# A chunk's k-blocks in twos: four high products in a row, then four low products

## The reference

```
x = x + 0.5 * SwiGLU_1(RMSNorm(x))
u = RMSNorm(x) @ w_in            # 2048 x 6144
   group A: differential attention, 4 heads; group B: stick-breaking attention, 8 heads
x = x + concat(A_out, B_out) @ w_out
x = x + 0.5 * SwiGLU_2(RMSNorm(x))
x = RMSNorm(x)
_swiglu(x) = (silu(x @ w_gate) * (x @ w_up)) @ w_down
```

## Time and profile before

| | us |
|---|---|
| median of 3 runs | 1893.87 |
| lowest run | 1893.20 |
| the profiled execution | 1893.42 |
| span of that execution, first to last instruction | 1891.6 |
| PE busy / its weight loads | 1875.1 / 1638.4 |
| DVE busy | 1133.5 |
| ACT busy | 902.9 |
| POOL busy | 16.7 |

### The profile page before, as it was taken

How to read it: one execution, slowest core, us unless ns; L and a number is a source line. 1 busy time by engine, 2 the same in 40 slices (tenths; PEclk the granted TensorE clock), 3 DMA queues, 4 the chain that set the end, 5 groups by cost and what they waited for, 6 DMA issues and landing times.

```text
span 1891.6 us, 28251 instructions
## 1 busy us (share of the span) xinstructions
PE 1875.1 (99%) x10792; PEld 1638.4 (87%) x10792; DVE 1133.5 (60%) x1303; ACT 902.9 (48%) x1213; POOL 16.7 (1%) x18
## 2 busy tenths in 40 slices
PE   8999999999999999999999999999999999999998
PEld 7888888888888888888888888888888888888887
DVE  7665556555555667565655566655555565556565
ACT  7444434444344446554656455444344444344454
POOL 0000000000000000100000000000000000000000
PEclk9999999999999999999999999999999999999999
DMA  9555655555555556554445555556555556655553
GB/s 306 180 197 181 197 178 195 184 197 180 181 196 186 186 167 216 179 173 162 157 161 172 172 185 180 197 182 196 178 195 183 197 179 187 191 192 185 176 172 119
DMA packets 344098, 349.91 MB, mean 185 GB/s; under 512 B 5984, under 2 KB 342112, under 8 KB 344032
## 3 DMA queue, kind: packets, MB, share of 16 engines
q1 hardware_dynamic: 343456, 348.02, 56.6%
q10 hardware_dynamic: 576, 0.96, 0.1%
HBM read 346.85 MB, written 2.10 MB: 184 GB/s over the span
## 4 chain that ended last, share of the span: by engine, by line
PE 61%; issue 38%; DVE 0%; DMA 0%; ACT 0%; POOLq 0%; POOL 0%; DVEq 0%
PE psum L1164 38%; PE psum L1169 19%; PE psum L1250 1%; PE psum L1253 0%; PE psum L1402 0%; DVE x_res L1118 0%; DMA param_sb<-in_params 0%; PE psum L1336 0%; PE psum L1347 0%; PE psum L1362 0%; PE psum L1393 0%; PE psum L1201 0%; PE psum L1394 0%; PE psum L1363 0%; PE psum L1346 0%
## 5 line engine op out<-in xcount | busy, mean ns | idle before, releaser
L1164 PE MATMUL psum<-x_split,w_split 128*128 128x512 f32 x3008 | 931.7, 395 | 0.0
L726 DVE TENSOR_TENSOR w_split<-w_raw,w_split 128x1024 fp32r<-128x1024 f32 (+1 forms) x664 | 766.5, 1196 | 252.3 <-ACT w_split L442 246.6
L442 ACT ACTIVATE w_split<-w_raw 128x1024 fp32r<-128x1024 f32 (+1 forms) x664 | 651.3, 1030 | 320.2 <-PE psum L1169 318.8
L1169 PEld LDWEIGHTS psum<-x_split,w_split 128*128 128x128 f32 x3008 | 551.8, 188 | 124.8
L1169 PE MATMUL psum<-x_split,w_split 128*128 128x256 f32 x3008 | 578.0, 279 | 0.0
L1164 PE MATMUL psum<-h_split,w_split 128*128 128x512 f32 x1640 | 507.1, 395 | 0.0
L1164 PEld LDWEIGHTS psum<-x_split,w_split 128*128 128x128 f32 x3008 | 465.4, 189 | 8.1
L1169 PEld LDWEIGHTS psum<-h_split,w_split 128*128 128x128 f32 x1640 | 300.4, 188 | 67.7
L450 ACT ACTIVATE lo_sum<-psum 128x512 f32<-128x512 f32 x159 | 95.0, 597 | 507.1 <-PE psum L1164 507.1
L1169 PE MATMUL psum<-h_split,w_split 128*128 128x256 f32 x1640 | 314.6, 279 | 0.0
L1164 PEld LDWEIGHTS psum<-h_split,w_split 128*128 128x128 f32 x1640 | 254.0, 189 | 4.8
(11 more groups left out here) (140 smaller groups left out, 530.9 us busy)
## 6 DMA issues: line engine op xcount, KB each, us to landing
w_raw<-in_ffn_gate SPq DMA_DIRECT2D x86, 1024.0 KB, 5.0
w_raw<-in_ffn_up SPq DMA_DIRECT2D x86, 1024.0 KB, 5.0
w_raw<-in_ffn_down SPq DMA_DIRECT2D x64, 1024.0 KB, 5.5
w_raw<-in_w_in SPq DMA_DIRECT2D x48, 1024.0 KB, 5.2
w_raw<-in_ffn_down SPq DMA_DIRECT2D x32, 768.0 KB, 4.8
w_raw<-in_w_out SPq DMA_DIRECT2D x16, 1024.0 KB, 5.5
x_res<-in_x_t SPq DMA_DIRECT2D x8, 256.0 KB, 6.9
w_raw<-in_ffn_gate SPq DMA_DIRECT2D x8, 256.0 KB, 7.0
```

Source lines behind the costliest of these rows:

```text
L442: nc.scalar.activation(w_split[:, slot % 2, 0, h * half:(h + 1) * half], w_raw[:, slot, h * half:(h + 1) * half], ACT.Copy).then_inc(hi_ma ...
L726: nc.vector.tensor_tensor(w_split[:, slot % 2, 1, part], w_raw[:, slot, part], w_split[:, slot % 2, 0, part].bitcast(F32), ALU.subtract).t ...
L1164: return mm(psum[:, 2 * j + b, :], one, other, start=first, stop=last)
L1169: return mm(psum[:, 2 * j + b, 256:512], one, other, start=False, stop=False)
```

## The change

`chunk` takes its k-blocks two at a time. For the k-blocks k0 and k0 + 1 it issues the four highs (k0 with b = 0 and 1, then k0 + 1 with b = 0 and 1), then the four lows in the same order. In the last pair of a strip's second chunk the four lows come first and the four highs last. `high` and `low` now take the k-block as an argument. The waits on `lo_made` by half and on `block_ready` are made at the even k-blocks; they stood there before as well, since `block_ready` names even k-blocks only and the halves start at even ones. `first_body` and `merged_chunk` are not touched.

```diff
--- before.py
+++ after.py
@@ -1149,34 +1149,34 @@
                 if not by_half:
                     pe.wait_ge(lo_made, lo_value(c))
                 w = w_split[:, slot % 2, :, 0:kn * STRIP].rearrange("p l (k n) -> p l k n", n=STRIP)
-                for k in range(kn):
-                    if by_half and k % (kn // 2) == 0:
-                        pe.wait_ge(lo_made, lo_value(c) - (k == 0))
-                    if block_ready is not None and block_ready(k) is not None:
-                        pe.wait_ge(*block_ready(k))
+
+                def high(k, b):
+                    cols = slice(b * P, (b + 1) * P)
                     a = left(k)
-                    first = not second and k == 0
-                    last = second and k == kn - 1
-
-                    def high(b):
-                        cols = slice(b * P, (b + 1) * P)
-                        one, other = (a[:, 0, cols], w[:, :, k, :]) if still else (w[:, 0, k, cols], a)
-                        return mm(psum[:, 2 * j + b, :], one, other, start=first, stop=last)
-
-                    def low(b):
-                        cols = slice(b * P, (b + 1) * P)
-                        one, other = (a[:, 1, cols], w[:, 0, k, :]) if still else (w[:, 1, k, cols], a[:, 0, :])
-                        return mm(psum[:, 2 * j + b, 256:512], one, other, start=False, stop=False)
-                    if last:
-                        low(0)
-                        low(1)
-                        high(0)
-                        ins = high(1)
+                    one, other = (a[:, 0, cols], w[:, :, k, :]) if still else (w[:, 0, k, cols], a)
+                    return mm(psum[:, 2 * j + b, :], one, other, start=not second and k == 0, stop=second and k == kn - 1)
+
+                def low(k, b):
+                    cols = slice(b * P, (b + 1) * P)
+                    a = left(k)
+                    one, other = (a[:, 1, cols], w[:, 0, k, :]) if still else (w[:, 1, k, cols], a[:, 0, :])
+                    return mm(psum[:, 2 * j + b, 256:512], one, other, start=False, stop=False)
+                for k0 in range(0, kn, 2):
+                    if by_half and k0 % (kn // 2) == 0:
+                        pe.wait_ge(lo_made, lo_value(c) - (k0 == 0))
+                    if block_ready is not None and block_ready(k0) is not None:
+                        pe.wait_ge(*block_ready(k0))
+                    four = [(k, b) for k in (k0, k0 + 1) for b in range(2)]
+                    if second and k0 == kn - 2:
+                        for k, b in four:
+                            low(k, b)
+                        for k, b in four:
+                            ins = high(k, b)
                     else:
-                        high(0)
-                        high(1)
-                        low(0)
-                        ins = low(1)
+                        for k, b in four:
+                            high(k, b)
+                        for k, b in four:
+                            ins = low(k, b)
                 ins.then_inc(chunk_used, 1)
 
             def x_block(second):
```

## The result

The changed kernel took 1900.84 us (median of 6 runs, 1900.40 to 1901.61) against 1893.71 for the kernel before (median of 6). The ratio is 1.0036, with a 95% interval of 1.0027 to 1.0046: slower, by 7.1 us between the medians, clear of the scatter and far inside the 2% that was named. One of the six runs of the kernel before took 10671.68 us and is left out of the ratio; without it that kernel's median is 1893.55. The forecast was 1903.7 with 1895 to 1915, a loss of 9.8 us.

A forecast was written before the change was run, and what follows sets the result against it. PE was taken as bound by distances between matmul starts. Span 1891.6 plus 9.8 us for lows and 0 for highs gave 1901.4, with 1.8 around it 1903.2; on the median of 1893.87, 1903.7 us, range 1895 to 1915.

The forecast's parts named there:

- PE's spacing is the bound, and nothing else moves.: On PE, distances between matmul starts set the time; the two old waits and the work of other engines stay.
- Count of long lows, 2580, at 0.1200 against 0.1162.: In chunks, 2580 more lows stand third or later in their row, at 0.1200 instead of 0.1162 us: 9.8 us.
- Highs: 0 ... I take 0, the value of the rows of four.: In chunks, highs in longer rows cost 0.2325 us each as in pairs: 0, with rows of eight -3 to +3 us.
- behind a high, a low or two start a little sooner: In rows of lows, the first two cost 0.1162 us each, and from the third on a low costs 0.1200.
- Rival 1: In rows of four lows, each low costs 0.1162 us, so nothing is added: 1893.9 us; chance 0.13.
- Rival 2: Between highs and lows, each switch costs 0.0287 us; 2580 fewer save 74 us, giving 1820; chance 0.01 beyond 2%.
- Rival 3: In rows of lows, third and later ones pay the whole 0.188 us load: 185 us, 2079 in all; chance 0.03 beyond 2%.
- Rival 4: In chunks, all lows cost 0.1200 us, also the first two of a row: 19.6 us more, 1913.5; chance 0.11.

The follow-up runs named there:

- 512-only: Against the kernel before, same order, each low moves 512 columns instead of 256 into the whole bank: 2434.27 us (2 runs).
- 256-only run: Against the kernel before, each high is two 256-column matmuls with a weight load each, save in a strip's first and last k-block: 1943.60 us, ratio 1.0261.

## Why the prediction was right, and where not

- **PE's spacing is the bound, and nothing else moves.** Right: same waits, same clock, same DVE and ACT.
- **Count of long lows, 2580, at 0.1200 against 0.1162.** The direction was right and the size too small: the lows lost 12.9 us, not 9.8. Part of that is the split of a period on the grid of 0.01 us: the 0.6974 of a period was right, but to the nanosecond two lows take 231.7 of it on the mean and two highs 465.9, not 232.4 and 465. The price by place in the row did not hold either. Rows of four lows in the kernel after come in kinds: the commonest, 471 ns, have places such as 118, 119, 117, 117, and 304 of 962 rows take 477 or 478 with the last three at 120. Only their mean, 473.3, is the forecast 472. That it came out is partly luck.
- **"Highs: 0 ... I take 0, the value of the rows of four."** This is the term that was mis-sized most: the highs gained 5.6 us. Eight highs take 1.84, not 1.86: about 0.02 x 150 = 3 us, the lower end of the bounds -3 to +3. The nearest rows, those of four, could not show it, since in this kernel the highs only fall to their floor after the fifth. The other half lies in rows of four against rows of two: 928 or 930 ns against 2 x 465.9 = 931.8. Where the period was split wrongly, what one side gains the other loses, so this cancels in the sum: with the eights alone the sum is 9.8 - 3 = 6.8, and 7.1 was measured.
- **The reading "behind a high, a low or two start a little sooner".** As a rule of prices it fitted the rows at hand, but it doesn't carry over to other orders. The 512-only and the 256-only run show the floors, 0.2266 and 0.120. Against them the highs of rows of two and four (0.2325) stand some 6 ns too high, the early lows 4 ns too low. A loss counted on lows alone forecasts more loss from longer rows (1908 and 1911), and these took 1892.85 and 1887.16.
- **Rival 1, nothing changes:** outside the interval, which begins at 1.0027.
- **Rival 2, the switch costs.** Its price was wrong, since the distance above the bare columns (512 and 256 at 2.4 GHz are 0.2133 and 0.1067 us) remains in kernels that never change width: 0.2266 - 0.2133 and 0.1200 - 0.1067 are both 13 ns a matmul. Its idea was half right: changing width does cost, but a change between fours costs over three times one between twos, so halving their number from there gained nothing. The argument against it, that a high costs the same in a four as in a two, was true to half a ns and didn't reach far enough: it says nothing on eights.
- **Rival 3** fell: 32 lows in a row stay at 0.120. **Rival 4**, all lows at 0.1200, is too high: it adds 19.6 us to the lows, and 12.9 were measured, nearer to the forecast's 9.8. In the third of the rows of four that take 477 or 478 ns it is almost right.

The Trainium skill, "TensorE: Matmul & The Clock Gate", section "Back-to-back issue gap", has N/2.4 plus 2.5 ns, 216 and 109 ns. No run here settles at them. With a weight load of its own for each matmul, the floors are 227 and 120.

**Open:** what holds the state between matmuls. The runs exclude the bank, the source of the weights and the place in the weight slots, and show that the widths and the order around a row decide. Why the alternation has a short and a long rhythm was only described, not explained. The traffic of the other engines was not varied by itself; against it as the cause speaks that 143 of the 148 rows of eight highs take 1840 or 1841 ns over the whole run.

## What to carry to other kernels

When PE waits for nothing, read the distances between starts over a whole period of the order, and get the floor of each width from a kernel that has only that width, before putting a loss down to one kind of matmul. Where matmuls of two widths can be regrouped, measure the longest rows that the accumulation allows against pairs, and don't infer the steps between from either: here rows of 32 gained 0.34%, pairs and eights were equal, and fours, halfway, lost 0.36%. A change's halves need not add up. A group's busy time on the page is no price, as it falls by the overlap when its members become neighbours.

## What was not expected of the hardware

- A 512-column matmul with a load of its own settles at 0.2267 us, but the first eight behind eight or more lows take 1.84, some 0.03 more than eight at the floor.
- High, low, high, low ran at 11.12 or at 11.28 to 11.29 us a strip, the same instructions and the same clock, in a fixed turn of three; exchanging two matmuls at each strip's end put every strip of the stretch at 11.30 and cost some 7 us over the kernel.
- Six highs took 1.37 us behind four lows, at the floor from the second on, and 1.39 behind six lows, at 228 to 236 ns each.
